# Where small groups of products stand beside the projection eighths in a stick-breaking attention loop, and where VectorE's root of k stands

## The reference

```python
q_a = heads_sb(rms_norm(sb_q.reshape(b, s, SB_HEADS, SB_HEAD_DIM), sb_q_norm_g[l]).reshape(b, s, SB_WIDTH))
k_a = heads_sb(rms_norm(sb_k.reshape(b, s, SB_HEADS, SB_HEAD_DIM), sb_k_norm_g[l]).reshape(b, s, SB_WIDTH))
o_sb = stick_breaking_attention(q_a, k_a, heads_sb(sb_v))
...
z = jnp.einsum('bhtd,bhsd->bhts', qb, kf) * scale
log_not = jnp.where(mask, jax.nn.log_sigmoid(-z), 0.0)
after = lax.cumsum(log_not, axis=3, reverse=True) - log_not
w = jnp.where(mask, jnp.exp(jax.nn.log_sigmoid(z) + after), 0.0)
return jnp.einsum('bhts,bhsd->bhtd', w, vf)
```

## Time and profile before

| | |
|---|---|
| median of three runs | 2238.01 us (2234.9 to 2240.77) |
| the profiled execution | 2237.48 us |
| its span, first to last instruction | 2235.5 us |
| mean granted clock of PE | 0.98 |
| busy: PE, DVE, POOL, ACT | 94%, 58%, 41%, 34% |
| the seven passes with a next pair | 577.24 to 1184.85 us |
| DMA | mean 69 GB/s |

### The profile page before, as it was taken

How to read it: one execution, slowest core, us unless ns; L and a number is a source line. 1 busy time by engine, 2 the same in 40 slices (tenths; PEclk the granted TensorE clock), 3 DMA queues, 4 the chain that set the end, 5 groups by cost and what they waited for, 6 DMA issues and landing times. The chain is left out here.

```text
span 2235.5 us, 30043 instructions
## 1 busy us (share of the span) xinstructions
PE 2109.9 (94%) x10120; PEld 1717.0 (77%) x10120; DVE 1286.5 (58%) x1863; ACT 760.7 (34%) x1329; POOL 911.3 (41%) x729
## 2 busy tenths in 40 slices
PE   3999999998999999999999699997899999999999
PEld 3788888887777777777777488885688888888887
DVE  4458686852457557566576565567644444444444
ACT  3233343311345445445445400003433222222232
POOL 3323231322333434433444233333855555555552
PEclk9999999999999999999999799999999999999999
DMA  3211121222431431432532452221211111011112
GB/s 107 47 38 48 34 56 24 62 68 73 98 87 27 103 80 42 103 67 55 103 55 72 176 187 87 78 70 47 76 57 46 48 56 48 29 54 56 56 56 75
DMA packets 137776, 153.85 MB, mean 69 GB/s; under 512 B 7664, under 2 KB 112112, under 8 KB 137728
## 3 DMA queue, kind: packets, MB, share of 16 engines
q1 hardware_dynamic: 136000, 150.07, 24.6%
q10 hardware_dynamic: 1728, 3.15, 0.4%
HBM read 107.06 MB, written 20.97 MB: 57 GB/s over the span
## 5 line engine op out<-in xcount | busy, mean ns | idle before, releaser
L123 POOL TENSOR_TENSOR w_hi<-w_raw,w_ones 128x64 fp32r<-128x64 f32 x88 | 38.8, 441 | 715.4 <-PE gla_g L147 315.3
L482 POOL TENSOR_TENSOR sb_rows<-sb_beta,sb_rest 128x128 f32<-128x128 f32 (+7 forms) x128 | 158.1, 1237 | 260.5 <-DVE sb_rest L837 244.6
L837 DVE TENSOR_TENSOR_SCAN sb_rest<-sb_rest 128x128 f32<-128x128 f32 (+7 forms) x128 | 210.1, 1645 | 34.9 <-ACT sb_beta L688 34.9
L126 POOL TENSOR_TENSOR w_lo<-w_raw,w_hi 128x1024 fp32r<-128x1024 f32 x88 | 216.6, 2461 | 7.3
L843 DVE TENSOR_TENSOR sb_wt_lo<-sb_t,sb_wt_hi 128x512 fp32r<-128x512 f32 x192 | 106.4, 554 | 171.0 <-ACT sb_wt_hi L696 170.2
L696 ACT CAST sb_wt_hi<-sb_t 128x512 fp32r<-128x512 f32 x192 | 92.3, 481 | 215.0 <-PE sb_t L581 213.8
L147 PE MATMUL sb_g<-h_hi,w_hi 128*128 128x512 f32 x544 | 161.7, 423 | 3.7 <-DVEq L741 3.7
L147 PE MATMUL sb_g<-h_lo,w_hi 128*128 128x512 f32 x544 | 155.3, 411 | 0.0
L147 PE MATMUL sb_g<-h_hi,w_lo 128*128 128x512 f32 x544 | 152.4, 404 | 0.0
L147 PE MATMUL gla_g<-h_hi,w_hi 128*128 128x512 f32 x480 | 129.4, 405 | 2.2 <-DVEq L1291 2.2
L147 PE MATMUL gla_g<-h_lo,w_hi 128*128 128x512 f32 x480 | 127.8, 399 | 0.0
(11 more groups left out here) (328 smaller groups left out, 5068.1 us busy)
## 6 DMA issues: line engine op xcount, KB each, us to landing
w_raw<-w_in SPq DMA_DIRECT2D x64, 512.0 KB, 8.1
ff_raw_g<-w_ffn_gate SPq DMA_DIRECT2D x11, 1024.0 KB, 5.4
ff_raw_u<-w_ffn_up SPq DMA_DIRECT2D x11, 1024.0 KB, 5.8
ff_raw_d<-w_ffn_down SPq DMA_DIRECT2D x11, 1024.0 KB, 4.8
sb_qs<-sb_q_st SPq DMA_DIRECT2D x32, 256.0 KB, 5.1
sb_kh<-sb_k_st SPq DMA_DIRECT2D x32, 256.0 KB, 5.0
sb_kl<-sb_k_st SPq DMA_DIRECT2D x32, 256.0 KB, 5.0
mp_sig<-gates_t SPq DMA_DIRECT2D x16, 512.0 KB, 4.3
```

The costliest lines, as they stand in the source:

```text
L123: self.nc.gpsimd.tensor_tensor(hi[:, 0:64], raw[:, 0:64], self.ones[:], ALU.mult)
L126: self.nc.gpsimd.tensor_tensor(lo, raw, hi, ALU.subtract).then_inc(self.ready, 1)
L482: nc.gpsimd.tensor_tensor(rows[tb // 4][:, tb % 4, 0:width], beta[:, n % 2, 0:width], rest[:, n % 2, 1:width + 1], ALU.mult).then_inc(row_ ...
L837: nc.vector.tensor_tensor_scan(back, back, back, 1.0, ALU.mult, ALU.bypass).then_inc(scanned, 1)
```

## The change

In PE's slots four groups are issued behind the eighth of their slot and ahead of `weigh`, instead of ahead of the eighth: the scores of slot 1 (`SCORE_AFTER`), the mean squares of slots 10 and 17 (`MS_AFTER`: second half of k and of q) and the spread of slot 18 (`SPREAD_AFTER`: second half). The mean squares of slots 6 and 13 and the spread of slot 14 stay ahead. On DVE the three parts of `k_root` go from slots 10, 11 and 12 to 11, 12 and 13; `repeat_k_rs` stays in slot 13, right behind the third part. In the last pass only the scores of slot 1 are concerned, and that slot has no eighth there.

```diff
+MS_AFTER = [10, 17]
+SPREAD_AFTER = 18
+SCORE_AFTER = 1
...
-                        if s in SCORE_SLOT:
+                        if s in SCORE_SLOT and s != SCORE_AFTER:
                             scores(it, SCORE_SLOT.index(s))
-                        if not last and s in MS_SLOT:
-                            i = MS_SLOT.index(s)
-                            mean_squares(it + 1, i // 2, i % 2, g_uses(it) + 2 * (i // 2) + 1)
-                        if not last and s in SPREAD_SLOT:
-                            spread_k_rs(it + 1, SPREAD_SLOT.index(s), g_uses(it) + 4)
+                        squares = lambda i: mean_squares(it + 1, i // 2, i % 2, g_uses(it) + 2 * (i // 2) + 1)
+                        spread = lambda i: spread_k_rs(it + 1, i, g_uses(it) + 4)
+                        if not last and s in MS_SLOT and s not in MS_AFTER:
+                            squares(MS_SLOT.index(s))
+                        if not last and s in SPREAD_SLOT and s != SPREAD_AFTER:
+                            spread(SPREAD_SLOT.index(s))
                         u, eighth = slot_of_unit(s - (LAST_LATER if last else 0))
                         if 0 <= u < fills:
                             fill(units(it), FIRST_UNITS + u, eighth, g_uses(it) + (u if last else (0, 2, 5, 6)[u]))
+                        if s == SCORE_AFTER:
+                            scores(it, SCORE_SLOT.index(s))
+                        if not last and s in MS_AFTER:
+                            squares(MS_SLOT.index(s))
+                        if not last and s == SPREAD_AFTER:
+                            spread(SPREAD_SLOT.index(s))
                         if done is not None:
                             weigh(it, done)
...
-                            if s in (10, 11, 12):
-                                k_root(it + 1, g_uses(it) + 1, s - 10)
+                            if s in (11, 12, 13):
+                                k_root(it + 1, g_uses(it) + 1, s - 11)
                             if s == 13:
                                 repeat_k_rs()
```

## The result

The changed kernel takes 2211.45 us (median of four runs, 2209.93 to 2212.94) against 2238.94 us for the kernel before in the same session: ratio 0.9873, 95% interval 0.986 to 0.9886. Its profiled execution took 2210.73 us, with a span of 2208.8 us. The forecast was 2213.5 us, range 2202 to 2229.

What follows compares the result with a forecast made beforehand. PE's idle time was taken as what can be won. Passes two to seven at 82.7 us and the first at 84.5 give 26.9 us less, net 24 after clock falls: 2237.5 - 24 = 2213.5 us, range 2202 to 2229.

Steps and rivals of the forecast that it cites:

- A: The forecast itself, the likeliest case: total of 2207 to 2219 us; chance 0.55.
- What bounds the loop: PE, busy 94% of the span; its largest gap, in slot 12, comes from VectorE's root held up by GpSimd's split.
- Slot 1: Scores behind the eighth no longer wait for `low_v`: gain 0.47 us a pass, none in the last; later scan priced at nothing.
- Slot 10: Mean squares behind the eighth no longer wait for `copy_k`: gain 1.11 us, with a new 0.2 us wait in slot 11.
- The root: Part 0, one slot later, waits for `w_lo` until 1128.84 and ends at 1129.85; slot 12's 2.78 us gap goes.
- New waits: PE waits 0.2 us in slot 11, 0.3 and 0.6 in slot 13, 0.45 in slot 14, 1.6 in slot 20.
- The sum for the pass: Seventh pass: 5.96 us of gaps gone, 3.15 us new, net 2.8 to 2.9; 85.6 becomes 82.7 us.
- The clock: In the loop, three falls of PE's clock remain at 1 us each; less than half of a fall shows.
- Rival B: VectorE isn't late in slot 20, so 1.6 us a pass stay won, 11 us more: 2202 us; chance 0.13.
- C: Root still costs VectorE 4.0 us in its new place; slots 12 to 20 come 1.3 us later: 2222.6 us; chance 0.20.
- D: Transposes of slot 13 take over slot 12's gap; only slot 1's 0.47 us are won: 2234 us; chance 0.08.
- E: Slower: new waits in slots 13, 14 and 20 let the clock fall, 5.1 us a pass: 2246 us; chance 0.04.

## Why the prediction was right, step by step

The likeliest case (A) came about; 2211.45 lies in its 2207 to 2219.

- *What bounds the loop* was right. The run with the root alone and the one with the short split show that slot 12's gap is GpSimd's split holding the root; the run with slot 10 alone shows that PE's time there is not on the path.
- *Slot 1*: 0.47 forecast, 0.6 measured for the pass when done alone. The cover held; no price for ScalarE or GpSimd.
- *Slot 10*: its 1.11 us were booked as won and partly as lost again (0.2 in slot 11). With the root moved, the pass with scores, slot 10 and root is 82.29 us, and with the root alone 83.04; less the 0.6 of slot 1 this leaves some 0.2 us for slot 10. The rest is taken back by the waits in slots 11 to 14 that I listed, which the run with the root alone doesn't have. The list was right, but a reader should see that it makes the part nearly worthless by itself.
- *The root*: part 0 was to end at 1129.85, which is 1104.48 in the times of after; the fifth instruction ended at 1104.36. The row of `w_lo` gave the right value between bounds of 1128.2 and 1131.2.
- *New waits*, idle plus 0.16: slot 11, 0.2 forecast, below what the profile shows in most passes; slot 13's transposes 0.3 forecast, 0.54 measured; its mean squares 0.6 forecast, 0.32 measured; the spread 0.45 forecast, about 0.2 (it starts at 1110.85, the copy ends at 1110.71, 0.5 earlier than forecast); slot 20, 1.6 forecast, 1.67 measured. Three terms were mis-sized, two of them too high. `low_q` ended 0.25 us earlier than forecast, and from there to the end of the copy it took 4.18 us instead of 4.45; GpSimd's row held one product of the root's last part in it (0.89 us).
- *The sum for the pass*: 82.7 forecast, 82.26 measured. The terms above, with the 0.6 us of slot 1, give a gain of about 3.1 of the 3.33 us; the other 0.2 I can't place.
- *The clock*: three falls at 1 us forecast in the changed kernel, none measured in the loop, in either profile of it. This term was wrong in kind. I judged by the length of idle time near narrow products; the gap of 1.5 us in slot 20 and the 0.9 us around slot 13 did not bring the clock down. The sentence that less than half of a fall shows is right for the pair behind slots 10 and 17 (0.8 us for two), but a stretch of 3.4 us at slot 12 shows with 1.1 to 1.4 of the 1.7 us that half the clock takes from PE. Together with the pass this makes the loop 5.4 us quicker than forecast (578.3 against 583.7).
- *Back to the total*: 2237.5 - 29.3 would have been 2208.2; stretches outside the loop, of which the prediction has no term, gave 2.6 us back in the profiled execution. So that the total lies within 3 us of the forecast is in part luck: the loop alone was off by 5.4.

Rival B (slot 20 shows no gap) was wrong: the gap is 1.51 us. C was wrong: part 0 takes 2.8 us in its new place (1101.56 to 1104.36) and not 4.0, because GpSimd's `w_hi` and 0.6 us of `w_lo` are past by then. D, that VectorE sets the pass as before, is what happens without the root's move, though the gap then stays in slot 12. E didn't occur; but the clock, its mechanism, costs the four groups alone more than slot 1 gives them, which I had not listed for them.

## What to carry to other kernels

When several engines walk the same slots, find for each gap of the bounding engine the queue that ends it, and ask where that queue is ahead again; only what shortens that queue counts, and two gaps that wait for one queue are one gap. Look for short instructions with long times beside another engine's long one: here a product on 16 elements cost 2.25 us and its place decided more than all four moved groups. And ask what stands behind a place where the clock falls: ahead of a wait for another engine a fall is partly paid out of that wait, at the gap itself it isn't.

## What the runs showed of the hardware that I had not expected

A conversion with a single SBUF input on 128x16 elements was held for 1.81 us by GpSimd's `w_lo`; with the split shortened it took 0.17 us in the same place of VectorE's program. PE's granted clock fell to 0.50 around the end of the single gap of 3.52 us in each of the seven passes with all four groups and the root as before, and in six of the seven with slot 10's mean squares alone; it stayed at 1.00 through all passes of the changed kernel, each with a gap of 1.5 us. A stretch of 3.4 us at the lower level cost 1.1 to 1.4 us at the gap of slot 12, and two of them behind slots 10 and 17 cost 0.8 us together.
